# Differential-attention scores in one fp32r pass: high and low parts of q and k stacked over the 128 rows, by way of DRAM

## The reference, cut to what matters

```python
def diff_attention(q, k, v, lam, lam_init, subln):
    scale = DA_HEAD_DIM ** -0.5                      # DA_HEAD_DIM = 32
    def block(qb):
        s = jnp.einsum('qbhid,bkhid->bhiqk', qb, k).astype(jnp.float32) * scale
        p = jax.nn.softmax(s, axis=-1)
        a = (p[:, :, 0] - lam * p[:, :, 1]).astype(v.dtype)
        return jnp.einsum('bhqk,bkhd->qbhd', a, v)
    o = map_query_blocks(block, q)
    o = rmsnorm(o, subln) * (1 - lam_init)
...
        k_all = jnp.concatenate([axial_rope(da_k), da_k_ctx.reshape(...)], axis=1)
        y_da = diff_attention(axial_rope(da_q), k_all, v_all, lam, lam_init, da_subln)
```

## Time and profile before

| | |
|---|---|
| median of 3 runs | 2910.71 us |
| the profiled execution, its time | 2910.96 us |
| its span, first to last instruction | 2909.2 us |
| PE busy | 2760.9 us, 95% |
| DVE, POOL, ACT busy | 1878.3, 1438.2, 980.7 us |
| mean granted TensorE clock | 0.974 of full speed |
| one layer's q and k strips (layer 0) | 561.9 to 618.5 us |
| v strips and 8 merge steps | 619.2 to 651.2 us |
| context units, latent units | 651.2 to 681.0, 681.0 to about 937 us |

### The profile page before, as it was taken

One profiled execution on the slowest core, in us unless ns is written; L12 is line 12 of the kernel. 1 busy time (PEld: TensorE's weight loads), 2 busy tenths in 40 slices (PEclk: granted clock), 3 DMA queues, 4 the chain that ended last, 5 costly groups with the idle time before them and its releaser, 6 DMA issues.

```text
span 2909.2 us, 43789 instructions
## 1 busy us (share of the span) xinstructions
PE 2760.9 (95%) x17224; PEld 2483.7 (85%) x17224; DVE 1878.3 (65%) x2941; ACT 980.7 (34%) x1843; POOL 1438.2 (49%) x620
## 2 busy tenths in 40 slices
PE   7879899999999998999998989999999998999998
PEld 2348777888888998999997969797988898999998
DVE  6456577674445558888886478565544565855866
ACT  3442112315655115242242112313565213422422
POOL 0425233283433774656665605065434575667554
PEclk9879998999999999999999999899999999999999
DMA  5422243141111432334222216032111331222222
GB/s 224 140 98 90 87 138 131 70 123 39 52 53 46 162 101 95 118 93 124 80 88 83 88 65 229 12 129 85 53 46 45 124 126 59 80 86 75 88 80 80
DMA packets 80537, 275.34 MB, mean 95 GB/s; under 512 B 9003, under 2 KB 14763, under 8 KB 78156
## 3 DMA queue, kind: packets, MB, share of 16 engines
q1 hardware_dynamic: 48124, 168.77, 18.8%
q10 hardware_dynamic: 32208, 103.77, 10.3%
HBM read 248.91 MB, written 23.59 MB: 94 GB/s over the span
## 4 chain that ended last, share of the span: by engine, by line
PE 74%; DVE 12%; ACT 5%; DVEq 4%; DMA 3%; issue 2%; POOLq 0%; POOL 0%; ACTq 0%; SPq 0%
PE PS L606 32%; PE PS L946 9%; PE PS L1086 7%; PE PS L667 4%; PE PS L995 3%; PE PS L741 2%; DVEq L2108 2%; DMA wraw<-in_w_strips 2%; PE PS L893 2%; DVE bsum L2109 2%; PE PS L616 1%; PE PS L967 1%; PE PS L877 1%; PE PS L707 1%; PE PS L829 1%
## 5 line engine op out<-in xcount | busy, mean ns | idle before, releaser
L574 POOL TENSOR_SCALAR whi<-wraw 128x1024 fp32r<-128x1024 f32 x188 | 550.3, 2927 | 982.9 <-PE PS L606 485.7
L576 POOL TENSOR_TENSOR wlo<-wraw,whi 128x1024 fp32r<-128x1024 f32 x212 | 552.8, 2608 | 90.1 <-ACT whi L1375 60.9
L1673 DVE CUSTOM_DVE_ANT_0 adap<-ada,cond 128x1024 f32<-128x1024 f32 x176 | 315.9, 1795 | 32.6 <-DMA ada<-in_w_ada 11.8
L606 PE MATMUL PS<-hhi,whi 128*128 128x320 f32 x1152 | 264.4, 311 | 11.6 <-POOL wlo L576 11.3
L606 PE MATMUL PS<-hlo,whi 128*128 128x320 f32 x1152 | 262.9, 309 | 0.0
L606 PE MATMUL PS<-hhi,wlo 128*128 128x320 f32 x1152 | 262.7, 309 | 0.0
L587 POOL TENSOR_TENSOR blo<-bsum,bhi 128x512 fp32r<-128x512 f32 x120 | 175.9, 1472 | 168.0 <-ACT bhi L1538 168.0
L2067 DVE SCALAR_TENSOR_TENSOR x<-PS,mod,x 128x128 f32<-128x128 f32 (+2 forms) x240 | 90.8, 433 | 177.5 <-PE PS L606 174.9
L606 PEld LDWEIGHTS PS<-hhi,whi 128*128 128x128 f32 x1152 | 192.4, 188 | 14.4 <-POOL wlo L576 12.6
L1086 PE MATMUL PS<-hhi,bhi 128*128 128x320 f32 x640 | 199.3, 311 | 1.6 <-POOL blo L587 1.0
L1086 PE MATMUL PS<-hhi,blo 128*128 128x320 f32 x640 | 197.7, 309 | 0.0
(11 more groups left out here) (335 smaller groups left out, 7276.5 us busy)
## 6 DMA issues: line engine op xcount, KB each, us to landing
wraw<-in_w_strips SPq DMA_DIRECT2D x292, 512.0 KB, 3.6
ada<-in_w_ada ACTq DMA_DIRECT2D x80, 512.0 KB, 4.9
spectra<-hst ACTq DMA_DIRECT2D x48, 256.0 KB, 2.1
cond<-conds ACTq DMA_DIRECT2D x7, 1024.0 KB, 7.2
hld<-spectra ACTq DMA_DIRECT2D x8, 768.0 KB, 5.1
hld<-spectra ACTq DMA_DIRECT2D x12, 512.0 KB, 3.7
part<-hacc ACTq DMA_DIRECT2D x8, 640.0 KB, 3.5
macc<-part ACTq DMA_DIRECT2D x8, 640.0 KB, 4.2
```

Source lines behind the costliest of these rows:

```text
L574: nc.gpsimd.tensor_scalar(hi, raw, 1.0, None, ALU.mult)
L576: nc.gpsimd.tensor_tensor(lo, raw, hi, ALU.subtract).then_inc(w_split, 1)
L606: ins = pe.matmul(out[:, h, :], w[:, kt, :], mv[:, h * HALF:(h + 1) * HALF], start=start and m == 0, stop=stop and m == 2)
L1673: ins = V.tensor_tensor_reduce(adap[s][:, :], ada[s][j][:, :], cond[s][:, c, :], 1.0, 0.0, ALU.mult, ALU.add, mraw[:, 2 * m + c:2 * m + c ...
```

## The change

q and k of the differential attention are split, after the rotation, into a high part (rounded to fp32r) and the low remainder. For each map of a head, a stack of 4 groups of 32 rows is formed: q as high, low, high, low and k as high, high, low, low. One matmul over 128 rows in fp32r then gives the sum of all four products. To move the groups to their rows, the parts are written to a DRAM tensor `dqk` and read back per head. The units now go head by head: unit n is head n // 5, block n % 5, so a context unit is followed by four latent ones; `steps_before` is adjusted (43 steps per head: 4, then 9 or 10). The stacks of heads 0 and 1 are read ahead of the loop, the others in the loop, two heads' worth of buffers in turn. The scores of a latent unit become two matmuls per map, cut at the PSUM bank border (384 and 256 columns, then 256 and 384). The whole-array zero padding of the cached keys goes away; they are split too and join the stacks.

```diff
+        dqk = nc.dram_tensor("dqk", [DEPTH, 2, KB, 4, 4, 32, T + C], F32, kind="Internal").ap()
...
         def steps_before(n):
-            return 8 + min(4 * n, 32) + max(0, (312 * (min(n, 40) - 8)) // 32)
+            h, qb = divmod(min(n, 40), NT)
+            return 8 + 43 * h + (4 + 39 * (qb - 1) // 4 if qb else 0)
...
                 v_strips(lay, S_DA + 8, s_nv)
                 pe.wait_ge(s_dcache, nth(lay, s_dcache, 32))
-                pe.wait_ge(s_drope, nth(lay, s_drope, 8))
...
                 def da_scores(n):
-                    qb, h = n // HEADS, n % HEADS
...
+                    h, qb = divmod(n, NT)
+                    if qb == 0:
+                        pe.wait_ge(s_st[h % 2], nth(lay, s_st[h % 2], 64 * (h // 2 + 1)))
...
+                    for m in range(2):
+                        q, k = dstq[h % 2][m][:, qb * 128:qb * 128 + 128], dstk[h % 2][m]
+                        first = DA_COL + DA_MAP * m
+                        if qb == 0:
+                            ins = pe.matmul(PSF[:, first + L:first + L + C], q, k[:, 0:C], start=True, stop=True)
+                        else:
+                            border = 512 * (m + 1) - first
+                            for lo, hi in ((0, border), (border, L + 128)):
+                                ins = pe.matmul(PSF[:, first + lo:first + hi], q, k[:, C + lo:C + hi],
+                                                start=True, stop=True)
...
# ACT, ahead of the loop
+                def stack_out(dst, src):
+                    act.dma_start(dst, src).then_inc(s_stw, 16)
+                def da_high(n, out):
+                    act.wait_ge(s_drope, nth(lay, s_drope, n + 1))
+                    act.wait_ge(s_stw, nth(lay, s_stw, 16 * out))
+                    A(dqhi[n % 2][:, :], drot[n % 2][:, :], ACT.Copy).then_inc(s_dhi, 1)
+                    if n >= 4:
+                        act.dma_start(a["new_da_k"][lay, :, n - 4, :], drot[n % 2][:, 0:C]).then_inc(s_ko, 16)
+                    act.wait_ge(s_dhi, nth(lay, s_dhi, n + 2))
+                    for g in ((0, 2), (0, 1))[n // 4]:
+                        stack_out(dqk[lay, n // 4, n % 4, :, g, :, 0:T], dqhi[n % 2][:, :].bitcast(F32))
+                def da_low_out(n):
+                    act.wait_ge(s_dlo, nth(lay, s_dlo, n + 2))
+                    for g in ((1, 3), (2, 3))[n // 4]:
+                        stack_out(dqk[lay, n // 4, n % 4, :, g, :, 0:T], dqlo[n % 2][:, :].bitcast(F32))
+                def stack_in(h):
+                    c, hm = h // 2, 2 * (h % 2)
+                    for m in range(2):
+                        for t, (st, cols) in enumerate(((dstq, T), (dstk, T + C))):
+                            act.dma_start(st[h % 2][m][:, :].bitcast(F32), dqk[lay, t, c, hm + m, :, :, 0:cols].rearrange(
+                                "g p n -> (g p) n")).then_inc(s_st[h % 2], 16)
+                act.wait_ge(s_dcache, nth(lay, s_dcache, 32))
+                A(dckhi[:, :, :], dck[:, :, :], ACT.Copy).then_inc(s_dhi, 1)
+                act.wait_ge(s_dlo, nth(lay, s_dlo, 1))
+                for c in range(KB):
+                    for t, src in enumerate((dckhi, dcklo)):
+                        for g in range(2 * t, 2 * t + 2):
+                            stack_out(dqk[lay, 1, c, :, g, :, T:T + C], src[:, c, :].bitcast(F32))
+                out = 16
                 for n in range(8):
...
                     A(halves(draw[n % 2][:, :]), pair((n + 3) % 4), ACT.Copy,
                       scale=-DA_SCALE if n < 4 else 1.0).then_inc(s_dqe, 1)
...
+                    if n >= 1:
+                        da_high(n - 1, out)
+                        out += 2
+                    if n >= 2:
+                        da_low_out(n - 2)
+                        out += 2
+                da_high(7, out)
+                for n in (6, 7):
+                    da_low_out(n)
+                act.wait_ge(s_stw, nth(lay, s_stw, 16 * (out + 6)))
+                for h in range(2):
+                    stack_in(h)
                 for k in range(4, KD):
                     ada_load(3, KD * lay + k, (lay, 2 * KD + k))
-                act.wait_ge(s_drope, nth(lay, s_drope, 8))
-                act.dma_start(a["new_da_k"][lay], dak[:, :, 0:C]).then_inc(s_ko, 16)
...
# ACT, in the loop
+                    if n % NT == 0 and NT <= n < 35:
+                        stack_in(n // NT + 1)
...
# DVE: dcklo = dck - dckhi ahead of the rotations; then, after each rotation into drot[n % 2]
+                def da_low(n):
+                    dve.wait_ge(s_dhi, nth(lay, s_dhi, n + 2))
+                    V.tensor_tensor(dqlo[n % 2][:, :], drot[n % 2][:, :], dqhi[n % 2][:, :], ALU.subtract).then_inc(s_dlo, 1)
...
                 modulation(lay, 2 * KD, N_ADA1)
+                dve.wait_ge(s_stw, nth(lay, s_stw, 16 * 48))
```

More of the change, by code:

```diff
@@ L79 @@
 MASK0 = [0, 2, 5, 8]
-DA_MAP = 896
+DA_MAP, DA_COL = 640, 128
 P_BADA, P_NMIX, P_NFFN, P_CW, P_CB, P_HB, P_END = 0, 48, 56, 64, 100, 112, 120
@@ L378, in build @@
         s_noT = sem("na_and_da_out_turned")
-        s_nyhi = sem("yna_hi_done")
-        s_yna = sem("yna_done")
-        s_dq = sem("da_qk_sum")
+        s_nyhi = sem("yna_and_yda_hi_done")
+        s_yna = sem("yna_and_yda_done")
         s_dqe = sem("da_qk_raw")
         s_drope = sem("da_rope")
-        s_dv = sem("da_v_sum")
-        s_dve = sem("da_v_kept")
+        s_dhi = sem("da_qk_hi")
+        s_dlo = sem("da_qk_lo")
+        s_stw = sem("da_stack_out")
+        s_st = [sem(f"da_stack_in{i}") for i in range(2)]
         s_dcache = sem("da_cache_in")
@@ L961, in da_scores @@
                     else:
[L962 to L973, removed]
+                        pe.wait_ge(s_nve, nth(lay, s_nve, NT + 5))
+                    for m in range(2):
[8 more added lines that the diff above has]
+                                                start=True, stop=True)
+                    ins.then_inc(s_ds, 1)
                 def da_turn(n):
@@ L1500, in _ @@
                     A(yda_hi[:, :, qb * 128:(qb + 1) * 128], PS[:, qb % 4, :].rearrange("p (c n) -> p c n", c=KB),
-                      ACT.Copy).then_inc(s_dyhi, 1)
+                      ACT.Copy).then_inc(s_nyhi, 1)
                 early_out(3)
@@ L1949, in _ @@
                     dve.drain()
-                    V.tensor_tensor(dst[:, n % 4, C:T], dst[:, n % 4, C:T], dsw[:, :], ALU.add).then_inc(s_drope, 1)
+                    V.tensor_tensor(dst[:, C:T], dst[:, C:T], dsw[:, :], ALU.add).then_inc(s_drope, 1)
+                    if n >= 1:
+                        da_low(n - 1)
                     if n in (1, 3, 5):
@@ L1958, in da_max @@
                 def da_max(n):
-                    p0, q = 0 if n // HEADS else 512, 2 * (n % 2)
-                    keys = 640 if n // HEADS else 128
+                    p0, q = DA_COL + (0 if n % NT else 512), 2 * (n % 2)
+                    keys = 640 if n % NT else 128
                     dve.wait_ge(s_ds, nth(lay, s_ds, n + 1))
@@ L2426 @@
         n[k] = g[k][0].reshape(DEPTH, 128, KB, 128).transpose(0, 3, 2, 1)
-    apart = np.zeros((DEPTH, 4, 32, KB, 4, 128), np.float32)
-    for m in range(4):
-        apart[:, m, :, :, m] = n["cache_da_k"][:, 32 * m:32 * m + 32]
-    n["cache_da_k"] = apart.reshape(DEPTH, 128, KB, 512)
     flat = g["na_rpb"].reshape(DEPTH, HEADS, 15 * 31)
```

83 lines of the change are left out of this document (45 added, 38 removed).

## The result

The changed kernel takes 3090.6 us (median of 4 runs, 3070.9 to 3092.7) against 2910.8 us: 1.060 times the time before, with a 95% interval of 1.0557 to 1.0646. It is slower by 180 us; the forecast was 3041 in a range of 2985 to 3140. The profiled execution took 3090.2 us, its span is 3088.4, so span against span it is 179.2 us longer.

The account below looks back on a forecast made before the run. PE was taken to set the pace in both the strips' stage and the loop. From 2911 us, 80 saved on PE and 210 lost on the way through DRAM (105 per layer) gave 3041, range 2985 to 3140.

Parts of the forecast that it names:

- The assumption that decided: Writes into dqk: a DMA is cut evenly along its outermost dimension, so outermost 4 runs on 4 engines; forecast had 78%.
- The bound of 7.0: Upper bound in us for one 328 KB write on 4 engines, from 11.7 GB/s per engine; 3.2 was taken.
- the rival of slow writes: Writes into dqk on four engines take 4.5 us and more each; 3156 us total at 5, 3284 at 7.0; chance 5%.
- The rounds: Layer 0's stage before the loop: rounds 2 to 7, four dqk writes each, take 16.3 us each, until 700.
- The start of the rounds: Layer 0's stage: cached values land, 16 cache writes take 17.6 us, and the rounds start at about 592.
- The tail: After the last round: stacks and modulation load 8.5 + 0.35 + 1.4 us, dots and modulation 18.9; first row maximum at 752.
- The clock: PE's clock drops to about half for 5 to 6 us after each of two long idles: 5 us per layer.
- The gain: PE's loop of units: 72 us from 64 latent units' scores and 8 from the 16 context units, together 80 us.
- the rival of the quarter rate: Narrow fp32r score matmuls run at a quarter rate, the gain is gone: 3138 us with four engines, 2943 with sixteen; 3%.
- "nothing": Stack loads in the loop, four per head issued by ACT, cost nothing, or up to 0.5 us x 12.
- The fast rival: All 16 engines serve the dqk writes, a round under 6 us, first maximum some 7 us late per layer: 2846 us; 14%.
- The lower end: Whole kernel: faster cache writes, no strip share, earlier loads, no clock loss and context gain 16 give about 2985 us.

Follow-up runs that it names:

- the mirror: Changed kernel with the DRAM buffer laid out four groups outermost, so writes have 128 rows in one piece and stack loads an outermost 4: 2948.5 us.
- With 128 rows: Changed kernel with the DRAM buffer laid out 128 rows by 4 groups, so each write and stack load has 128 rows outermost: 2891.7 us.
- the order alone: Kernel before with units head by head and steps spread as in the change, scores as before, no way through DRAM: 2906.0 us.
- the later runs: Follow-ups to the changed kernel, among them 128-row buffer with modulation loads moved (2874.9 us), plus cached keys in four DMAs (2865.0), plus loads earlier still (2857.7).

## Why the prediction held, and where it was off

**The assumption that decided.** That a DMA into a pattern whose outermost dimension is 4 runs on four engines was read from one transfer of 33 rows that had 11 completions. It holds: by the count of 10507 packets, by a DMA share of 0.26, and by three runs that change how the same bytes are cut (3091 to 2892 and to 2975; the mirror, where the loads have the 4, at 2949). This agrees with what the Trainium skill says of the number of engines ("DMA: Bandwidth & Descriptors", the section on why a DMA increments its semaphore by 16), now at 4 as well as at 11, and on the source side of a load as on the target side of a write.

**The rate.** 3.2 us per write on 4 engines: 82 KB at 104 / 4 = 26 GB/s per engine is 3.15. The bound of 7.0 was far off, and so was the rival of slow writes.

**The rounds** are the term that was too small. From the second high copy at 603.8 to the eighth at 721.4 they took 117.7 us, against 98 forecast. Four writes at full rate account for 12.6 us of 18.2. I had 3.5 for the rest, with 0.7 for the copy, 0.35 for an issue, 1.4 for completion and 1 for the strip. It was 5.6, though PE idled and no strip shared the engines. What I left out is a slow start: over the five microseconds after 642 the engines move 160 KB where 104 GB/s would be 520, which is 3.5 us lost, and the copy and the first issue are only 1.3 of it. Why the start is slow stays open. ACT hands out the writes one by one (0.53, 0.53, 1.5 us), but a single one already is 3.2 us of work for its four engines. The two rounds that overlap the v strips took 21.2 and 22.0. With the first round (13.0 instead of 10) and the last (24.4 instead of 22.7), and a start 1.2 us early, this is 23 us of the stage. So the eighth draw copy came at 682.9 instead of 668, and PE's wait was 65 us, not 49.

**The start of the rounds** was right by luck. I had the first high copy wait until the 16 writes of cached keys had landed, at 592. It came at 590.8, but behind DVE's first rotation: ACT's first draw copy stood behind the issuing of those writes, 15.2 us from 569.6 to 584.8, and the rotation behind the copy.

**The tail** gave 4 us back. Stacks and first modulation load took 12.6 us for 10.3, but dots and modulation 12.4 instead of 18.9: I had moved durations measured beside a busy POOL (1.2 to 3.2 us a dot, the shown one 1.83) into a stretch in which POOL has nothing to do (1.23 each). That POOL is the cause fits these numbers; no run took its work away by itself. The sum of both: 23 - 4 = 19, and the first maximum came 119 us late per layer, not 100.

**The clock.** 5 us per layer were forecast. After the first wait the granted clock is 0.50, 1.2 of 2.4 GHz, for 4 us, and the first nine v matmuls start 0.43 us apart instead of 0.23. After the second it is 0.50 until 776.5. And it falls a third time in the loop, from 933 to 940 us, after PE's wait of 3.4 us for the early sum:

```profile
936.00:938.00 2.00, 2.00 (x11) 1.96 (x9) 2.00 (x3) 0.21 (x1) 0.00 (x0) 0.50 0.00 0
```

Over the stretches of 1 us in the v strips and the loop, the share of the clock that PE was not granted adds up to 8.3 us in layer 0 and 8.4 in layer 1, of which 6.2 and 5.7 lie in the loop. But the kernel before lost 3.4 and 1.7 in its own loops, which the forecast didn't take off. The change adds 11.6 us for both layers, against 10: the size was right, the parts were not.

**The gain** was 65 us instead of 80. The scores themselves are as forecast, 0.58 us for 0.59, and fp32r matmuls of 256 and 384 columns run at the rate of the wide ones; the rival of the quarter rate falls. With 128 rows the loops give 71 us: 10 from the order, forecast 8, and 61 from the scores, forecast 72.

- The order's 10 us come by another way than I said. PE waits 2.3 and 2.8 us less in the loops, and the clock's 3.4 and 1.7 us are not lost in this run: 10.2 together. So the 8 was right in size only.
- PE's own work fell by more than 36 us per layer: 1.14 us in each of 32 latent units, and the two score matmuls of a context unit cost 0.23 us instead of 0.61, together 39.5. Against the order alone, PE then waits 7.2 and 5.2 us longer and loses 1.7 and 4.4 us to the clock. That leaves 30.6 and 29.9; measured are 30.6 and 30.9.
- The step that failed is "nothing" for the stack loads in the loop, and that only the waits of the earlier trace rows stay. In layer 0 the new waits are 3.3 us for the early sum, which lands in 9.2 us behind a head's four stack loads where it took 3.5 in the median of the earlier trace rows, 2.1 instead of 0.8 for DVE's difference, and 1.6 for an exp.
- The 6 us by which the changed kernel's loops are longer than those with 128 rows are about the clock's: 11.9 against 6.1 us lost. The loops of the later runs, 266.5 to 271.8 us, differ in part for the same reason: where layer 0 took 270.7 and 271.4 us, about 8 us went to the clock.

In sum: 210 lost and 80 gained were forecast, 238 and 65 came, and 6 us lie elsewhere in the program: 2909.2 + 238 - 65 + 6 = 3088 us of span. That 3091 lies inside the range owes something to luck: its upper part was made of writes of 4.2 us and slow cache writes, which didn't come, and the slow start of each round took their place.

**The fast rival** said 2846 with 16 engines, and the run of 128 rows gave 2892. Sixteen engines for the writes is what that run has, but two prices of the rival were wrong. Its gain of 80 was 71. And its first maximum was to be 7 us late and came 20 and 24 us late. In layer 0 most of this is the rounds: the rival had the last write landed some 65 us after the start of the stage, and it was 81. The stacks and the first modulation load took 14.1 us for 10.3, the dots and the modulation 14.2 for 18.9.

**Sums of the forecast.** Four times 0.59 is 2.4 us, not 2.1, so the rival of the quarter rate would have given 3154 with four engines, above the range. The lower end adds up to 2989. With 2.0 us for each completion, ten of them in a layer's chain, the sum would be 12 us higher, not 10. None of this changes the forecast.

The Trainium skill gives the fixed part of a DMA, about 2.0 us ("DMA: Bandwidth & Descriptors", the section "Anatomy of one DMA"), for DMAs that GpSimd issues, a condition that the forecast left out. For those that ACT issues here it is less: pieces of 80 KB over 16 engines land in 1.8 us (median), 0.2 of it transfer at 406 GB/s, so 1.6.

## What to carry to other kernels

Count engines before bytes: the completions on the page (its packets under 512 B, less those of rows that are really so short), divided by the number of DMAs, tell how many engines a transfer really had, and a buffer of one's own can be laid out so that both sides have 128 rows outermost. A detour that is hidden in bytes can still end a stage through the queue that issues it: what stands behind it on that queue (here loads with two slots) must be moved ahead in the same change. And when PE's stream gets denser, look for the small transfers and copies that were just covered before, above all for those that are now issued behind new loads on the same queue.

## What the runs showed that I hadn't expected

- An issue on ACT's queue takes 0.33 to 0.55 us with little outstanding, but 1.4 to 4.0 in the changed kernel's last round and 9.2 us in the mirrored one with five four-engine loads ahead. ACT does nothing else in that time, so a narrow DMA costs its issuer too.
- Four engines need 4 to 5 us from the first issue of a round to reach their 104 GB/s, in the rounds begun at 642.6 and 660.8 us.
- A head's stack loads delay the small write that is issued behind them. The early sum lands after 9.2 us with loads on 16 engines and after 17.3 with loads on four, though the bytes are the same, and PE's wait for it goes from 3.3 to 7.3 us in layer 0. Of the 8.1 us more, 3.6 are ACT's longer issue.
- A long idle cost PE's clock no more than a short one here. After 65 us without work the granted clock was 0.50 for 4 us (683.6 to 687.6); in the kernel before, after a wait of 1.5 us, it was 0.50 for 6.7 us (656.8 to 663.5).
